# Up weights in whole rows with 512-column matmuls, and each expert's down product after its successor's gate and up products

## Chip, cores and metric

One core of one Trainium2 chip runs the whole layer as one program. The metric is the device time of one execution in microseconds. A change under about 0.5% (8 us) can't be told from none.

## What is computed

One trunk layer: token mixing (mLSTM and GLA scans, an input and an output projection), then expert-choice routed SwiGLU experts. The change touches only the experts. From the reference, cut:

```python
aff = jax.nn.softmax(jnp.einsum('bnd,de->bne', h, w_router).astype(jnp.float32), axis=-1)
g, idx = lax.top_k(jnp.swapaxes(aff, 1, 2), cap)          # cap = 128 tokens for each of 16 experts
xin = jax.vmap(lambda hb, ib: hb[ib])(h, idx)
hid = jax.nn.silu(jnp.einsum('becd,edf->becf', xin, w_gate)) * jnp.einsum('becd,edf->becf', xin, w_up)
y = jnp.einsum('becf,efd->becd', hid, w_down) * g[..., None].astype(h.dtype)
return jax.vmap(lambda yb, ib: jnp.zeros((n, d), h.dtype).at[ib.reshape(-1)].add(yb.reshape(-1, d)))(y, idx)
```

Model width and expert width are 1024. Each expert so has three fp32 matrices of 4 MB, 12 MB in all, and works on 128 tokens, one tile of partitions.

## The kernel before

Every product is made of three fp32r matmuls: each operand is split in a high part (a copy in fp32r) and a low part (operand less high part), and high x high, high x low and low x high are summed in PSUM. The token side is stationary (128x128), the weights move through.

**Units.** An expert's weights come in 12 units of 1 MB (`EU = 12`): units 0 to 3 are gate, 4 to 7 up, 8 to 11 down. Gate and down units are 256 whole rows of the matrix (2 rows of 4 KB for a partition). An up unit is 256 columns of all 1024 rows (8 pieces of 1 KB for a partition). SyncE (SP) loads unit u of the next expert into `e_raw[u]` as soon as TensorE has used unit u of this one; the semaphore `w_used` counts used units. There are 12 raw buffers, so a load has 12 units of time before its own matmuls.

**Splits.** ScalarE (ACT) copies a unit to its high part (`e_split_hi`, L958) into one of 4 buffers (`EH = 4`), so it must wait until the unit four places earlier was used. VectorE (DVE) then writes the low part over the raw unit (`e_split_lo`, L1440). Both run in an order that is written out by hand (`expert_act`, `expert_dve`).

**TensorE's order** (`expert_pe`, L1846): gate units (48 matmuls of 512 columns, L1829), up units (96 matmuls of 256 columns, L1820 to L1822, one quarter of the hidden width per unit), in between the transposes of finished quarters of `hid` (L1843, 8 in all), the 8 transposes of the next expert's tokens (L1836), then the down units (48 matmuls of 512 columns). A quarter of `hid` is multiplied by its up product as soon as its unit is done (`hid_part`), transposed, and split (`hd_hi_part`, `hd_lo_part`), while TensorE works on the next quarter. At the end ACT scales the result into `y_exp` (L989).

**GpSimd (POOL)** gathers the next expert's tokens by an indirect DMA and adds each result to the accumulator in DRAM by another (`scatter`); `y_taken` tells that `y_exp` may be written again. After the last scatter the accumulator is read back, normalised and added to the stream.

The loop over experts is a hardware loop of 15 rounds with the last expert written behind it. The order of an expert in TensorE's program is

```python
for u in range(4):
    e_unit(e, u, xt_hi, xt_lo, e_ps(0))
for q in range(4):
    e_unit(e, 4 + q, xt_hi, xt_lo, quarter(2, q))
    if q:
        hid_transposes(e, q - 1)
if not last:
    x_transposes(e + 1)
hid_transposes(e, 3)
pe.wait_ge(y_free, e + 1)
for u in range(8, EU):
    pe.wait_ge(hd_ok, 4 * e + u - 8 + 1)
    e_unit(e, u, hd_hi, hd_lo, e_ps(4))
```

Of the kernel before, what the change touches and what calls it, by code (L numbers as in the profile page):

```python
# [97 lines left out]
EH = 4  # L98


def build(nc, I, out):

    ctx = ExitStack()
    with ctx:
# [352 lines left out]
        def _(sp):  # L457
# [52 lines left out]
            def expert_src(e, u):  # L510
                if 4 <= u < 8:
                    c = slice(UW * (u - 4), UW * (u - 3))
                    return I["w_e_up"][ds(e, 1), :, c].rearrange("o (k p) n -> p (o k) n", p=P)
                w = I["w_e_gate"] if u < 4 else I["w_e_down"]
                r = 2 * P * (u % 4)
                return w[ds(e, 1), r:r + 2 * P, :].rearrange("o (k p) n -> p (o k) n", p=P)

            def load_expert_unit(e, u):
                dst = e_raw[u][:].rearrange("p (k n) -> p k n", k=KC if 4 <= u < 8 else 2)
                sp.dma_start(dst, expert_src(e, u)).then_inc(e_full[u], 16)  # L520
# [37 lines left out]
        def _(pool):  # L558
# [103 lines left out]
        def _(act):  # L662
# [292 lines left out]
            def e_split_hi(e, u):  # L955
                act.wait_ge(e_full[u], 16 * e + 16)
                act.wait_ge(w_used, EU * e + u + 1)
                act.activation(e_hi[u % EH][:], e_raw[u][:], ACT.Copy).then_inc(e_hi_ok, 1)  # L958

# [4 lines left out]
            def hd_hi_part(e, q):  # L964
                act.wait_ge(hd_mm, 4 * e + q + 1)
                act.activation(hd_hi[:, 2 * q:2 * q + 2, :], quarter(0, q).rearrange("p (k n) -> p k n", k=2), ACT.Copy).then_inc(hd_hi_ok, 1)

            def e_split_his(e, units):
                for u in units:
                    e_split_hi(e, u)  # L970

            def expert_act(e, last):
                act.wait_ge(w_used, EU * e + 4 + EH)
                act.activation(hid[:], e_ps(0), ACT.Silu).then_inc(sg_ok, 1)
                e_split_his(e, (7, 8))
                hd_hi_part(e, 0)
                e_split_hi(e, 9)
                hd_hi_part(e, 1)
                e_split_hi(e, 10)
                hd_hi_part(e, 2)  # L980
                if not last:
                    xt_hi_part(e + 1)
                hd_hi_part(e, 3)
                e_split_hi(e, 11)
                if not last:
                    e_split_his(e + 1, range(3))
                act.wait_ge(w_used, EU * e + EU + EH)
                act.wait_ge(y_taken, e + 1)
                act.activation(y_exp[:], e_ps(4), ACT.Copy, scale=gates[:, ds(e, 1)]).then_inc(y_free, 1)  # L989
                if not last:  # L990
                    e_split_his(e + 1, range(3, 7))
# [9 lines left out]
            e_split_his(0, range(EH, 7))
            with act.Fori(0, N_EXP - 1) as e:
                expert_act(e, False)
            expert_act(N_EXP - 1, True)
# [10 lines left out]
        def _(dve):  # L1015
# [431 lines left out]
            def hid_part(e, q):  # L1447

                if q == 0:
                    dve.wait_ge(sg_ok, e + 1)  # L1450
                dve.wait_ge(w_used, EU * e + 4 + q + 1 + EH)
                h = hid[:, UW * q:UW * (q + 1)]
                dve.tensor_tensor(h, h, quarter(2, q), ALU.mult).then_inc(hid_ok, 1)

            def hd_lo_part(e, q):
                dve.wait_ge(hd_hi_ok, 4 * e + q + 1)
                dve.tensor_tensor(hd_lo[:, 2 * q:2 * q + 2, :], quarter(0, q).rearrange("p (k n) -> p k n", k=2),
                                  hd_hi[:, 2 * q:2 * q + 2, :], ALU.subtract).then_inc(hd_ok, 1)

            def e_split_los(e, units):  # L1460
                for u in units:
                    e_split_lo(e, u)

            def expert_dve(e, last):
                hid_part(e, 0)
                e_split_lo(e, 7)
                hid_part(e, 1)
                e_split_lo(e, 8)
                hd_lo_part(e, 0)
                hid_part(e, 2)  # L1470
                e_split_lo(e, 9)
                hd_lo_part(e, 1)
                hid_part(e, 3)
# [470 lines left out]
```

## Time and profile before

| | us |
|---|---|
| median of 3 runs | 1591.79 |
| lowest and highest | 1586.74, 1592.2 |
| the profiled execution | 1591.46 |
| its span, first to last instruction | 1589.7 |
| expert stage, TensorE's first to last matmul of experts | 979.6 to 1544.6 |

The profile is of one execution; its times are us from the start of its span. "PEclk" or the granted clock is the share of TensorE's full 2.4 GHz that it was given; the other level is 0.5, or 1.2 GHz. PE is TensorE's matmuls, PEld its weight loads. The chain of waits follows the work that ended last back through what released each step, so a stall of TensorE shows in it as a step of another engine or of a DMA. A DMA share over 1 comes from packets that overlap on an engine.

### The profile page before, as it was taken

How to read it: one execution, taken by the hardware profiler on the slowest of the kernel's cores; microseconds unless marked ns; L12 is line 12 of the kernel's file. 1: busy time of each engine (PE TensorE's matmuls, PEld its weight loads, DVE VectorE, ACT ScalarE, POOL GpSimd, SP SyncE). 2: the span in 40 equal slices, each digit the busy share in tenths (PEclk: the TensorE clock that was granted, in tenths of full speed). 3: DMA queues.
4: the chain of work that ended last, by engine and by line, in shares of the span. 5: the costliest groups of instructions: out<-in, count | busy, mean ns of one | idle time of the engine just before them, and what ended most of it. 6: DMA issues, size and time to landing. Idle time of an engine off the chain costs nothing.

```text
span 1589.7 us, 21961 instructions
## 1 busy us (share of the span) xinstructions
PE 1344.7 (85%) x8140; PEld 1180.9 (74%) x8140; DVE 1023.0 (64%) x1325; ACT 765.1 (48%) x853; POOL 103.7 (7%) x121
## 2 busy tenths in 40 slices
PE   4786999899699998178789934999999999999980
PEld 1775889789589997057468823998888889988870
DVE  5637431299534461666734466888888888888855
ACT  5624321133210112466422231877878788787742
POOL 1000000110000000100200001000001000000103
PEclk9998999999899999579799966999999999999995
DMA  9911023000353342000031192999999999999965
GB/s 343 262 38 37 27 62 98 0 1 0 106 185 107 107 133 106 0 1 0 1 119 40 40 331 89 351 380 375 374 374 378 374 373 381 380 380 380 375 199 222
DMA packets 151506, 299.21 MB, mean 188 GB/s; under 512 B 4816, under 2 KB 104144, under 8 KB 149472
## 3 DMA queue, kind: packets, MB, share of 16 engines
q1 hardware_dynamic: 144688, 273.34, 47.4%
q0 software_dynamic: 6768, 25.17, 6.3%
q8 instruction: 36, 0.59, 0.1%
q14 instruction: 14, 0.11, 0.0%
HBM read 277.52 MB, written 29.36 MB: 193 GB/s over the span
## 4 chain that ended last, share of the span: by engine, by line
PE 38%; issue 12%; DVE 2%; DMA 2%; ACT 1%; SPq 1%; POOL 1%; POOLq 0%; DVEq 0%; ACTq 0%
PE psum L1829 21%; PE psum L1822 4%; PE psum L1821 4%; PE psum L1820 4%; PE psum L1707 1%; PE psum L1715 1%; SPq L520 1%; PE psum L1726 1%; PE psum L1725 1%; PE psum L1836 1%; DMA e_raw<-w_e_up 1%; PE psum L1843 1%; PE psum L1741 1%; DVE ht_f L1296 1%; POOL diag L629 1%
## 5 line engine op out<-in xcount | busy, mean ns | idle before, releaser
L1440 DVE TENSOR_TENSOR e_lo<-e_raw,e_hi 128x2048 fp32r<-128x2048 f32 x192 | 434.1, 2287 | 47.5 <-ACT e_hi L958 46.4
L958 ACT ACTIVATE e_hi<-e_raw 128x2048 fp32r<-128x2048 f32 x192 | 362.7, 1913 | 65.5 <-PE psum L1829 50.0
L1613 PE MATMUL psum<-w_hi,h_hi 128*128 128x256 f32 x576 | 165.3, 287 | 0.5 <-issue 0.5
L1615 PE MATMUL psum<-w_lo,h_hi 128*128 128x256 f32 x576 | 164.5, 286 | 0.0
L1614 PE MATMUL psum<-w_hi,h_lo 128*128 128x256 f32 x576 | 164.5, 286 | 0.0
L1820 PE MATMUL psum<-e_hi,xt_hi 128*128 128x256 f32 x512 | 147.3, 288 | 0.0
L1822 PE MATMUL psum<-e_lo,xt_hi 128*128 128x256 f32 x512 | 144.8, 283 | 0.0
L1821 PE MATMUL psum<-e_hi,xt_lo 128*128 128x256 f32 x512 | 144.7, 283 | 0.0
L1613 PEld LDWEIGHTS psum<-w_hi,h_hi 128*128 128x128 f32 x576 | 112.2, 195 | 0.6 <-issue 0.6
L1614 PEld LDWEIGHTS psum<-w_hi,h_lo 128*128 128x128 f32 x576 | 112.3, 195 | 0.0
L1615 PEld LDWEIGHTS psum<-w_lo,h_hi 128*128 128x128 f32 x576 | 112.1, 195 | 0.0
L1821 PEld LDWEIGHTS psum<-e_hi,xt_lo 128*128 128x128 f32 x512 | 98.1, 192 | 0.6
L1820 PEld LDWEIGHTS psum<-e_hi,xt_hi 128*128 128x128 f32 x512 | 97.9, 191 | 0.6
L1572 PE MATMUL psum<-h_hi,w_hi 128*128 128x512 f32 x224 | 72.5, 406 | 30.4 <-DVE kT L1117 14.0
L1822 PEld LDWEIGHTS psum<-e_lo,xt_hi 128*128 128x128 f32 x512 | 97.9, 191 | 0.0
L1829 PE MATMUL psum<-e_hi,xt_hi 128*128 128x512 f32 x256 | 80.0, 394 | 2.5 <-DVE xt_lo L1444 2.5
L1829 PE MATMUL psum<-e_hi,hd_hi 128*128 128x512 f32 x256 | 80.3, 395 | 0.0
L1829 PE MATMUL psum<-e_hi,xt_lo 128*128 128x512 f32 x256 | 79.7, 393 | 0.0
L1829 PE MATMUL psum<-e_lo,xt_hi 128*128 128x512 f32 x256 | 79.7, 393 | 0.0
L1829 PE MATMUL psum<-e_lo,hd_hi 128*128 128x512 f32 x256 | 79.0, 390 | 0.0
L1829 PE MATMUL psum<-e_hi,hd_lo 128*128 128x512 f32 x256 | 78.9, 389 | 0.0
L1572 PE MATMUL psum<-h_lo,w_hi 128*128 128x512 f32 x224 | 71.4, 400 | 0.0
(352 smaller groups left out, 2619.8 us busy)
## 6 DMA issues: line engine op xcount, KB each, us to landing
e_raw<-w_e_gate SPq DMA_DIRECT2D x64, 1024.0 KB, 16.2
e_raw<-w_e_up SPq DMA_DIRECT2D x64, 1024.0 KB, 13.5
e_raw<-w_e_down SPq DMA_DIRECT2D x64, 1024.0 KB, 13.3
ada_x<-w_ada SPq DMA_DIRECT2D x16, 1024.0 KB, 5.3
raw<-w_in_units SPq DMA_DIRECT2D x15, 1024.0 KB, 4.9
ada_raw<-w_ada SPq DMA_DIRECT2D x8, 1024.0 KB, 12.1
xs<-x SPq DMA_DIRECT2D x4, 1024.0 KB, 13.9
acc_dram<-zero_r SPq DMA_DIRECT2D x1, 4096.0 KB, 19.0
```

Source lines behind the costliest of these rows:

```text
L520: sp.dma_start(dst, expert_src(e, u)).then_inc(e_full[u], 16)
L629: pool.tensor_tensor(diag[:], ident[:].unsqueeze(1).to_broadcast([P, KC, P]), vec_c[:, q, :].unsqueeze(2).to_broadcast([P, KC, P]), ALU.mu ...
L958: act.activation(e_hi[u % EH][:], e_raw[u][:], ACT.Copy).then_inc(e_hi_ok, 1)
L1440: dve.tensor_tensor(e_lo[u][:], e_raw[u][:], e_hi[u % EH][:], ALU.subtract).then_inc(e_lo_ok, 1)
L1572: last = pe.matmul(t_lat(s)[:, BANK * q:BANK * (q + 1)], w[m][:, k, c], h[:, k, CTX + BANK * q:CTX + BANK * (q + 1)], start=a, stop=z)
L1613: pe.matmul(o, x_hi[:, k, c], w_hi[n % 2][:, k, :], start=k == 0, stop=False)
L1614: pe.matmul(o, x_lo[:, k, c], w_hi[n % 2][:, k, :], start=False, stop=False)
L1615: last = pe.matmul(o, x_hi[:, k, c], w_lo[n % 2][:, k, :], start=False, stop=k == KC - 1)
L1820: pe.matmul(o, x_hi[:, k, :], hi[:, c], start=k == 0, stop=False)
L1821: pe.matmul(o, x_lo[:, k, :], hi[:, c], start=False, stop=False)
L1822: i = pe.matmul(o, x_hi[:, k, :], lo[:, c], start=False, stop=k == KC - 1)
L1829: i = pe.matmul(o[:, BANK * b:BANK * (b + 1)], x[:, k, :], w[:, D * j + BANK * b:D * j + BANK * (b + 1)], start=a, stop=z)
```

## The change

Up units become pairs of whole rows as gate and down have, and their matmuls get 512 columns. With that, the up product is finished only with its last unit, so there are no quarters any more: `hid` is multiplied, transposed and split in one piece each. TensorE's order is turned: gate and up of expert e, token transposes of e + 1, down of e - 1, `hid` transposes of e. Expert 0 has no down before it and stands ahead of the loop; the last expert's down stands behind it. The loads follow the order of use, and the scatter of expert e is issued behind the gather of e + 3 where it was e + 1.

```diff
             def expert_src(e, u):
-                if 4 <= u < 8:
-                    c = slice(UW * (u - 4), UW * (u - 3))
-                    return I["w_e_up"][ds(e, 1), :, c].rearrange("o (k p) n -> p (o k) n", p=P)
-                w = I["w_e_gate"] if u < 4 else I["w_e_down"]
+                w = (I["w_e_gate"], I["w_e_up"], I["w_e_down"])[u // 4]
...
-            with sp.Fori(0, N_EXP - 1) as e:
-                for u in range(EU):
-
-                    sp.wait_ge(w_used, EU * e + u + 1 + EH)
+            for u in range(8):
+                sp.wait_ge(w_used, u + 1 + EH)
+                load_expert_unit(1, u)
+            with sp.Fori(1, N_EXP - 1) as e:
+                for u in range(8):
+                    sp.wait_ge(w_used, EU * e - 4 + u + 1 + EH)
                     load_expert_unit(e + 1, u)
+                for u in range(8, EU):
+                    sp.wait_ge(w_used, EU * e - 4 + u + 1 + EH)
+                    load_expert_unit(e, u)
+            for u in range(8, EU):
+                sp.wait_ge(w_used, EU * (N_EXP - 1) - 4 + u + 1 + EH)
+                load_expert_unit(N_EXP - 1, u)
...
-            with pool.Fori(1, N_EXP) as e:
+            for e in (1, 2):
                 pool.wait_ge(xt_mm, e)
                 gather(e, tok_g_ok, e)
-                scatter(e - 1)
-            scatter(N_EXP - 1)
+            for e in range(3, N_EXP):
+                pool.wait_ge(xt_mm, e)
+                gather(e, tok_g_ok, e)
+                scatter(e - 3)
+            for e in range(N_EXP - 3, N_EXP):
+                scatter(e)
...
+            def expert_act(e):
+                n = EU * e - 4
+                up_his(e, n + 4)
+                gate_silu(e, n)
+                down_his(e - 1, n + 8)
+                xt_hi_part(e + 1)
+                gate_his(e + 1, n + EU)
+                y_part(e - 1, n + 8)
+                hd_hi_part(e)
...
+            def expert_dve(e):
+                n = EU * e - 4
+                lows(4, n + 4)
+                lows(8, n + 8, range(3))
+                hid_part(e, n)
+                lows(8, n + 8, (3,))
+                xt_lo_part(e + 1)
+                lows(0, n + EU)
+                hd_lo_part(e)
...
+            gate_up(0, 0)
+            x_transposes(1)
+            pe.wait_ge(xt_ok, 2)
+            hid_transposes(0)
+            with pe.Fori(1, N_EXP - 1) as e:
+                n = EU * e - 4
+                gate_up(e, n)
+                pe.wait_ge(hd_ok, e)
+                x_transposes(e + 1)
+                down(e - 1, n + 8)
+                pe.wait_ge(xt_ok, e + 2)
+                hid_transposes(e)
+            last = EU * (N_EXP - 1) - 4
+            gate_up(N_EXP - 1, last)
+            down(N_EXP - 2, last + 8)
+            hid_transposes(N_EXP - 1)
+            down(N_EXP - 1, last + EU)
```

**Two places in the order of the engines.** First ACT, from the last expert's SiLU to the end of the experts; before (L958 is a weight unit's high part with the buffer and raw unit named, L966 the high part of `hid`, L989 the result):

```order
L974 ACTIVATE hid_190<-psum 128x1024 [waits w_used]
L958 ACTIVATE e_hi3_186<-e_raw7_166 128x2048 [waits w_used,e_full7]
L958 ACTIVATE e_hi0_183<-e_raw8_167 128x2048 [waits w_used,e_full8]
L966 ACTIVATE hd_hi_191<-psum 128x256 [waits hd_mm]
L958 ACTIVATE e_hi1_184<-e_raw9_168 128x2048 [waits w_used,e_full9]
L966 ACTIVATE hd_hi_191<-psum 128x256 [waits hd_mm]
L958 ACTIVATE e_hi2_185<-e_raw10_169 128x2048 [waits w_used,e_full10]
L966 ACTIVATE hd_hi_191<-psum 128x256 [waits hd_mm] x2
L958 ACTIVATE e_hi3_186<-e_raw11_170 128x2048 [waits w_used,e_full11]
L989 ACTIVATE y_exp_193<-psum,gates_195 128x1024 [waits y_taken,w_used]
```

The same stretch after the change, in which units 8 to 11 come twice, first those of expert 14 and then those of expert 15:

```order
L978 ACTIVATE hid_190<-psum 128x1024 [waits w_used]
L962 ACTIVATE e_hi0_183<-e_raw8_167 128x2048 [waits w_used,e_full8]
...
L962 ACTIVATE e_hi3_186<-e_raw11_170 128x2048 [waits w_used,e_full11]
L962 ACTIVATE e_hi0_183<-e_raw8_167 128x2048 [waits w_used,e_full8]
L962 ACTIVATE e_hi1_184<-e_raw9_168 128x2048 [waits w_used,e_full9]
L962 ACTIVATE e_hi2_185<-e_raw10_169 128x2048 [waits w_used,e_full10]
L962 ACTIVATE e_hi3_186<-e_raw11_170 128x2048 [waits w_used,e_full11]
L991 ACTIVATE y_exp_193<-psum,gates_195 128x1024 [waits y_taken,w_used]
L986 ACTIVATE hd_hi_191<-psum 128x1024 [waits hd_mm]
L991 ACTIVATE y_exp_193<-psum,gates_195 128x1024 [waits y_taken,w_used]
```

The high part of `hid`, which stood between the down units in quarters, now stands behind all four down units of its own expert and behind the result of the expert before.

Second TensorE, from the end of expert 0's up product onwards (L1829 and L1839 are the matmuls of 512 columns, L1843 and L1852 the `hid` transposes, L1836 and L1846 the token transposes). Before, behind the last quarter's matmuls:

```order
L1843 MATMUL psum<-ident_50,hid_190 128x128 [waits hid_ok]
L1843 MATMUL psum<-ident_50,hid_190 128x128
L1834 ISA
L1836 MATMUL psum<-ident_50,x_tok_187 128x128 [waits gathered]
L1836 MATMUL psum<-ident_50,x_tok_187 128x128 x7
L1840 REGISTER_ALU
L1843 MATMUL psum<-ident_50,hid_190 128x128 [waits hid_ok]
L1843 MATMUL psum<-ident_50,hid_190 128x128
L1815 REGISTER_ALU [waits hd_ok,y_free]
L1829 MATMUL psum<-e_hi0_183,hd_hi_191 128x512 [waits e_lo_ok]
```

and after:

```order
L1839 MATMUL psum<-e_hi3_186,xt_lo_189 128x512 x2
L1846 MATMUL psum<-ident_50,x_tok_187 128x128 [waits gathered]
L1846 MATMUL psum<-ident_50,x_tok_187 128x128 x7
L1852 MATMUL psum<-ident_50,hid_190 128x128 [waits hid_ok,xt_ok]
L1852 MATMUL psum<-ident_50,hid_190 128x128 x7
L1874 UNCONDITIONAL_BRANCH
L1874 ISA
L1832 ISA [waits xt_ok]
L1839 MATMUL psum<-e_hi0_183,xt_hi_188 128x512 [waits e_lo_ok]
```

Before, the down product of expert 0 follows the transposes; after, no matmuls stand between expert 0's up product and expert 1's gate product but the two sets of transposes.

## Rows read from the trace of the kernel before

**Rows 1.** The page: busy totals, and granted clock in 40 slices.

```profile
PE 1344.7 (85%) x8140; PEld 1180.9 (74%) x8140; DVE 1023.0 (64%) x1325; ACT 765.1 (48%) x853; POOL 103.7 (7%) x121
...
PEclk9998999999899999579799966999999999999995
```

**Rows 2.** Windows view: stretch, its us, busy us (instructions), granted clock, DMA share, GB/s.

```profile
1200.00:1400.00 200.00, 200.00 (x1204) 179.16 (x1203) 177.35 (x124) 159.45 (x116) 16.54 (x22) 1.00 1.05 377
```

**Rows 3.** Chain of waits, one expert: start, us, what.

```profile
1212.43 0.22 PE psum L1843 x2
1215.52 0.22 PE psum L1843 x2
1215.74 0.87 PE psum L1836 x8
...
1216.83 21.80 PE psum L1829 x96
...
1251.87 4.34 PE psum L1829 x19
```

**Rows 4.** Groups by form, 1100:1300: busy us, mean ns of one, idle before.

```profile
L1440 DVE TENSOR_TENSOR e_lo<-e_raw,e_hi 128x2048 fp32r<-128x2048 f32 x69 | 156.0, 2287 | 12.8 <-ACT e_hi L958 12.4
L958 ACT ACTIVATE e_hi<-e_raw 128x2048 fp32r<-128x2048 f32 x69 | 130.2, 1913 | 16.6 <-PE psum L1829 16.6
...
L1453 DVE TENSOR_TENSOR hid<-hid,psum 128x256 f32<-128x256 f32 x24 | 10.1, 421 | 10.2 <-PE psum L1822 8.1
...
L1444 DVE TENSOR_TENSOR xt_lo<-psum,xt_hi 128x1024 fp32r<-128x1024 f32 x6 | 7.3, 1214 | 0.0
L989 ACT ACTIVATE y_exp<-psum,gates 128x1024 f32<-128x1024 f32 x6 | 6.7, 1119 | 5.3 <-PE psum L1829 5.3
...
L962 ACT ACTIVATE xt_hi<-psum 128x1024 fp32r<-128x1024 f32 x6 | 6.2, 1028 | 2.9 <-PE psum L1836 2.9
```

**Rows 5.** Windows view: loads of 1 KB pieces, of 4 KB rows, scatter, gather.

```profile
1328.00:1338.00 10.00, 10.00 (x46) 8.29 (x45) 8.05 (x4) 8.01 (x5) 1.78 (x2) 1.00 1.10 348
1341.00:1344.00 3.00, 3.00 (x17) 2.53 (x16) 2.63 (x2) 2.93 (x2) 0.00 (x0) 1.00 1.03 270
1351.00:1353.00 2.00, 2.00 (x20) 2.00 (x19) 1.86 (x4) 1.09 (x2) 0.00 (x0) 1.00 1.03 412
1354.00:1362.00 8.00, 8.00 (x49) 7.12 (x49) 7.87 (x8) 6.32 (x6) 0.00 (x0) 1.00 1.03 410
```

**Rows 6.** Timeline of SP's load issues: start, us, what.

```profile
1336.93 9.56 SPq L520 DMA_DIRECT2D e_raw<-w_e_gate  x4
...
1483.16 8.97 SPq L520 DMA_DIRECT2D e_raw<-w_e_gate  x4
```

**Rows 7.** Load issue to landing: one at 985.3, all of 1300:1400.

```profile
e_raw<-w_e_gate SPq DMA_DIRECT2D x1, 1024.0 KB, 5.0
...
DMA to landing us min/median/max: 11.6/19.1/21.4
```

**Rows 8.** Chain of waits, last two experts.

```profile
1462.08 21.79 PE psum L1829 x96
...
1508.92 13.87 DMA e_raw<-w_e_up
...
1533.64 10.91 PE psum L1829 x48
```

**Rows 9.** Timeline of PE: first work after a gap, gap in brackets.

```profile
69.01 1.31 PE L1536 MATMUL psum<-ident,xs 128*128 128x128 f32 x10 [2.25 <-ACT h L726]
```

**Rows 10.** Windows view: the clock behind gaps of PE.

```profile
70.40:73.80 3.40, 3.04 (x13) 2.65 (x14) 3.37 (x4) 2.47 (x4) 0.00 (x0) 0.50 1.14 208
84.10:90.80 6.70, 5.69 (x16) 4.72 (x17) 6.63 (x6) 4.41 (x4) 0.00 (x0) 0.50 0.01 1
411.20:415.10 3.90, 3.90 (x11) 3.22 (x12) 3.87 (x2) 0.00 (x0) 0.00 (x0) 0.50 0.02 4
415.10:419.00 3.90, 3.90 (x22) 3.32 (x21) 1.82 (x2) 1.91 (x1) 0.00 (x0) 1.00 0.52 147
```

More of the change, by code:

```diff
@@ L962, in xt_hi_part, with hd_hi_part, y_part @@
                 act.activation(xt_hi[:].rearrange("p k n -> p (k n)"), e_ps(6), ACT.Copy).then_inc(xt_hi_ok, 1)
[L964 to L987, printed above, removed]
+            def hd_hi_part(e):
+                act.wait_ge(hd_mm, e + 1)
+                act.activation(hd_hi[:].rearrange("p k n -> p (k n)"), e_ps(6), ACT.Copy).then_inc(hd_hi_ok, 1)
+            def y_part(e, n):
+                act.wait_ge(w_used, n + 4 + EH)
                 act.wait_ge(y_taken, e + 1)
                 act.activation(y_exp[:], e_ps(4), ACT.Copy, scale=gates[:, ds(e, 1)]).then_inc(y_free, 1)
-                if not last:
-                    e_split_his(e + 1, range(3, 7))
+            def expert_act(e):
[7 more added lines that the diff above has]
+                hd_hi_part(e)
             all_stored(act)
@@ L997, in _ @@
             act.nop().then_inc(y_free, 1)
-            e_split_his(0, range(EH))
+            gate_his(0, 0)
             act.wait_ge(route_ready, 1)
             xt_hi_part(0)
[L1001 to L1004, printed above, removed]
+            up_his(0, 4)
+            gate_silu(0, 0)
+            xt_hi_part(1)
+            gate_his(1, 8)
+            hd_hi_part(0)
+            with act.Fori(1, N_EXP - 1) as e:
+                expert_act(e)
+            last = EU * (N_EXP - 1) - 4
+            up_his(N_EXP - 1, last + 4)
+            gate_silu(N_EXP - 1, last)
+            down_his(N_EXP - 2, last + 8)
+            down_his(N_EXP - 1, last + EU)
+            y_part(N_EXP - 2, last + 8)
+            hd_hi_part(N_EXP - 1)
+            y_part(N_EXP - 1, last + EU)
             for j in range(4):
@@ L1460, in e_split_los @@
[L1460 to L1473, printed above, removed]
-                e_split_lo(e, 10)
-                hd_lo_part(e, 2)
-                if not last:
-                    xt_lo_part(e + 1)
-                hd_lo_part(e, 3)
-                e_split_lo(e, 11)
-                if not last:
-                    e_split_los(e + 1, range(7))
@@ L1483, in _, with hid_part, hd_lo_part @@
-            e_split_los(0, range(3))
-            xt_lo_part(0)
-            e_split_los(0, range(3, 7))
-            with dve.Fori(0, N_EXP - 1) as e:
-                expert_dve(e, False)
-            expert_dve(N_EXP - 1, True)
+            def hid_part(e, n):
+                dve.wait_ge(sg_ok, e + 1)
+                dve.wait_ge(w_used, n + 8 + EH)
+                dve.tensor_tensor(hid[:], hid[:], e_ps(2), ALU.mult).then_inc(hid_ok, 1)
+            def hd_lo_part(e):
+                dve.wait_ge(hd_hi_ok, e + 1)
+                dve.tensor_tensor(hd_lo[:].rearrange("p k n -> p (k n)"), e_ps(6), hd_hi[:].rearrange("p k n -> p (k n)"),
+                                  ALU.subtract).then_inc(hd_ok, 1)
@@ L1490, in _ @@
+            last = EU * (N_EXP - 1) - 4
+            lows(4, last + 4)
+            lows(8, last + 8, range(3))
+            hid_part(N_EXP - 1, last)
+            lows(8, last + 8, (3,))
+            lows(8, last + EU)
+            hd_lo_part(N_EXP - 1)
             for j in range(4):
@@ L1844, in hid_transposes, with gate_up @@
                 i.then_inc(hd_mm, 1)
[L1846 removed]
+            def gate_up(e, n):
                 pe.wait_ge(xt_ok, e + 1)
                 for u in range(4):
[L1849 to L1856 removed]
+                    e_unit(u, n + u, xt_hi, xt_lo, e_ps(0))
+                for u in range(4):
+                    e_unit(4 + u, n + 4 + u, xt_hi, xt_lo, e_ps(2))
@@ L1857, in expert_pe, with down @@
+            def down(e, n):
                 pe.wait_ge(y_free, e + 1)
-                for u in range(8, EU):
-                    pe.wait_ge(hd_ok, 4 * e + u - 8 + 1)
-                    e_unit(e, u, hd_hi, hd_lo, e_ps(4))
+                pe.wait_ge(hd_ok, e + 1)
+                for u in range(4):
+                    e_unit(8 + u, n + u, hd_hi, hd_lo, e_ps(4))
             pe.wait_ge(route_ready, 1)
             x_transposes(0)
-            with pe.Fori(0, N_EXP - 1) as e:
-                expert_pe(e, False)
```

94 lines of the change are left out of this document (43 added, 51 removed).

## Prediction

> **What bounds the kernel now.** I read the views in this order. The page's busy totals [rows 1] say little, as they mix all stages: PE 85%, DVE 64%, ACT 48%. The slices show that from 985 us on the granted clock stays full (the last 9s of PEclk), which is the expert stage. A window in that stage [rows 2] shows PE busy for all of its 200 us at clock 1.00, DVE for 177 and ACT for 159, and the DMA engines at a share of 1.05. So TensorE sets the pace, but the DMA has hardly a margin. The chain of waits over one expert [rows 3] holds TensorE alone, without a gap: 96 matmuls of gate and down take 21.80 us (0.2271 each), 8 token transposes 0.87, 8 `hid` transposes 0.87 in four pieces, and the expert lasts 1251.87 - 1216.83 = 35.04 us. That leaves 11.50 for the 96 up matmuls; a single quarter gives the same, 1215.52 - 1212.43 - 0.22 = 2.87 for 24, or 0.1196 each.
>
> Whether the DMA keeps up is read from the loads. From 1336.93 to 1483.16 SP issues four experts' loads [rows 6], 36.56 us for each, slower than TensorE's 35.04. Issue to landing grows from 5.0 us for the first load of the stage to a median of 19.1 around 1350 [rows 7]. This backlog lives on the 12 raw buffers, and runs out only in the last experts: in the chain [rows 8] the last down product starts at 1533.64 and the one two experts earlier at 1462.08, 71.56 us apart, where two experts take 70.08, less 0.87 for token transposes that the last one lacks: 69.21. So 2.4 us are lost to late loads, and the chain goes through a load of an up unit (13.87 us from 1508.92).
>
> **Part 1, up matmuls of 512 columns.** 96 of 256 columns go, 11.50 us, and 48 of the form of gate and down come, 48 x 0.2271 = 10.90. On a TensorE that never waits the whole 0.60 us counts, for 16 experts **-9.6 us**. The number of transposes stays.
>
> **Part 2, up loads of 4 KB rows.** The windows [rows 5] show loads in 1 KB pieces at 348 GB/s and in 4 KB rows at 410, so 3.01 us and 2.56 us for 1 MB. Four units save 1.8 us an expert: 36.6 goes to 34.8 for the DMA. TensorE's new expert is 35.04 - 0.60 = 34.44. The DMA stays behind by 0.4 us an expert, 6 us over the stage, against the 1.5 x 14 = 21 us that the buffers took before the first stall. So the late loads go: **-2.4 us** (between -2.4 and 0).
> The Trainium skill speaks against this part: "DMA: Bandwidth & Descriptors", Specifications, gives 512 B as the smallest transfer for line rate, by which 1 KB and 4 KB rows would load equally fast. Here they don't (348 against 410 GB/s). What the rule would make of the time is rival A.
>
> **Part 3, the turned order, within the loop.** TensorE waits for nothing if each low part is ready before its unit. Set 0 at the start of gate(e); a unit takes 12 x 0.2271 = 2.73 us. Down units start at 22.7, `hid` transposes at 33.6, gate(e + 1) at 34.44. ACT makes a high part (1.91 us [rows 4]) when the unit four places earlier is used; SiLU follows gate at 10.9, the last down high part starts at 21.9 when the last up unit is used. DVE (2.29 a low part) has eleven low parts and this expert's product behind the up units: three down units' low parts done by 24.1, `hid_part` until 25.3, the fourth low part until 27.6 where TensorE needs it at 30.9, xt_lo until 28.8, and gate(e + 1)'s first low part at 31.1, needed at 34.44. The smallest margin is so 3.2 us. DVE's sum is 12 x 2.29 + 3 x 1.21 = 31.1 of 34.44 us, ACT's 12 x 1.91 + 3 x 1.03 + 1.12 = 27.2. `hid_part` over 1024 columns isn't in the trace: 1.21 as xt_lo, at most 4 x 0.42 = 1.68 as four quarters. The margin covers both, so this part costs **0**. Behind `y_part` on ACT stand `hd_hi` and the first up high part, whose parts TensorE reads 17 and 3.3 us after they are done. On POOL the scatter of e - 3 stands behind the gather of e, which has waited for the transposes of the round before; the next gather is needed a whole round later. The new waits of TensorE on `hd_ok` and `xt_ok` end 17 and 5 us before they are reached.
>
> **Part 4, the start.** Here the cover is gone: expert 0 has no down of a predecessor [the second order excerpt]. From the end of up(0) at 0: token transposes until 0.87, xt_hi 1.03 until 2.1 (hand-offs of 0.03 to 0.2 included), xt_lo 1.21 until 3.3; only then may the `hid` transposes write the same PSUM banks, 3.4 to 4.3. ACT makes the first high part of gate(1) behind xt_hi, 2.1 to 4.0, DVE its low part until 6.3; TensorE starts gate(1) at 6.4. The later units come every 2.29 us, faster than the 2.73 they are used in. TensorE waits 2.6 + 2.1 = **+4.7 us** (4 to 6).
>
> **Part 5, the end.** Down(15) follows down(14) with only the `hid` transposes between. Two things meet. The loads of down(15) go into the buffers of down(14), each when its unit is used, which in the loop is 12 units ahead of use and here 4. And ACT has its four high parts in front of `y_part(14)` and of `hd_hi(15)` [the first order excerpt]; `hd_hi(15)` is what TensorE waits for. From the end of down(14) at 0: the last load is issued, and the DMA has nothing else, so it lands at 5.0 [rows 7]; its high part until 6.9, y_part 1.12 until 8.1, hd_hi 1.03 until 9.1; DVE ends the low part at 9.2, hd_lo until 10.4; with hand-offs TensorE goes on at 10.9, where its transposes ended at 0.87: **+10.0 us**. Were the load no wait, the high part would end at 2.1 and the gap be 4.9; that is the lower bound, 11.5 with a landing of 6.5 the upper. The scatter of expert 14 has 16 us until y_part(15) writes `y_exp` again, and behind down(15) all is as before.
>
> **The clock.** Before, the stage has no gap. In other stages the clock fell behind gaps: 2.25 us of gap ahead of 69.01 [rows 9], and 70.4 to 73.8 shows 0.50, the 1.2 GHz level; 84.1 to 90.8 also shows 0.50, and 411.2 to 415.1 right behind idle time, where 11 matmuls run in 3.9 us and 22 in the next 3.9 at 1.00 [rows 10]: half the time at this level is lost. At the end I take 3.9 us of low clock behind the 10 us gap, **+2.0** (1.5 to 2.8). At the start the gaps are 2.6 and 2.1 us with 0.9 of transposes between; **+2.0**, between 0 and 3.4 (half of 6.7).
>
> **Sum.** 1591.46 - 9.6 - 2.4 + 4.7 + 10.0 + 2.0 + 2.0 = 1598.2. The profiled execution is 0.3 us under the median of the runs, 1591.79, so nothing is added. The forecast is **+6.4 us, 0.4%**: the saving of 16 experts is given back in two gaps. Differences under 0.5% (8.0 us, so below 1599.8) can't be told from none by such a measurement.
>
> **Rivals.**
> A, slower: the loads stay at 36.56 us an expert. Against 34.44 the DMA falls behind by 2.1 an expert, 32 us in 15; the buffers bear 21, so TensorE loses 11 where before it lost 2.4. Time 1598.2 + 11 = 1609. It decides once an expert's loads take over 34.44 + 21 / 15 = 35.8. Against it stand the 348 and 410 GB/s; for it that gather and scatter (270 GB/s while the scatter runs [rows 5]) stay. Chance 0.08.
> B, slower: a wait in each round, because DVE does its product for `hid` in the middle of the down low parts. It decides when over 3.2 us come on top; 1 us a round then gives 1598.2 + 15 = 1613. For it: DVE is 90% busy and in order. Chance 0.07.
> C, no change: the two gaps are shorter, the clock stays up at the start and the last load doesn't matter: 1598.2 - 2.0 - 5.1 = 1591. Chance 0.15.
> D, faster: both ends are hidden and only the savings stay, 1591.46 - 12.0 = 1579.5. Nothing covers a TensorE that has no other product to run, so 0.05.
> The forecast itself, 1594 to 1603: 0.65, of which 0.2 lies over 1599.8.
>
> **Numbers.** Slower by over 0.5%: 0.08 + 0.07 + 0.20 = 0.35. Within: 0.45 + 0.15 = 0.60. Faster: 0.05. The range takes in the lower half of no case below C and reaches over the forecast to near A: 1590 to 1607. The likeliest case's own is 1594 to 1603.
>
> **What would show it.** An expert's period of 34.4 us with up matmuls 0.227 apart; load issue to landing that stays well under 19 us; a DMA rate in loads of 410 GB/s throughout; two gaps of TensorE on xt_lo and e_lo behind expert 0, 2.6 and 2.1 us; one of 10 us ahead of the last down product, released by hd_lo (L1477) with hd_hi behind a load of down; clock 0.50 behind both. Wrong would be: a period over 34.6 (A if it grows late and ACT waits for loads, B if from the first round), or an end gap of 5.

## The result

Eleven runs of the changed kernel have a median of 1598.73 us (1593.02 to 1599.7), eleven of the kernel before on the same chip 1589.64 (1584.26 to 1592.2). The ratio is 1.0056 with a 95% interval of 1.0042 to 1.0069: slower by 9 us, on the edge of what the measurement can tell from nothing. The profiled execution took 1598.76 us, the forecast was 1598.2. The ratio is formed over all the runs and can differ from the quotient of the medians, by up to 0.1% in the table of experiments.

### The profile after

The page, with the same lines as [rows 1]:

```profile
PE 1343.1 (84%) x7372; PEld 1146.5 (72%) x7372; DVE 1019.7 (64%) x1229; ACT 744.4 (47%) x791; POOL 123.2 (8%) x121
...
PEclk9888999999899999579799966999999999999985
```

TensorE has 768 matmuls less and is as busy as before (1343.1 us for 1344.7). The last two digits of the clock, 85 for 95, are a first sign of what happened at the end.

The windows view, as [rows 2] (us, busy us and instructions of PE, PEld, DVE, ACT, POOL, then granted clock, DMA share, GB/s), and the landings of the same stretch as in [rows 7]:

```profile
1200.00:1400.00 200.00, 200.00 (x932) 166.56 (x931) 178.79 (x88) 154.20 (x94) 27.36 (x24) 1.00 1.03 398
```

```profile
DMA to landing us min/median/max: 6.4/8.0/8.7
```

TensorE still never waits within the loop. The DMA engines move 398 GB/s where they moved 377, and a load lands 8.0 us after its issue where it took 19.1: the backlog is gone.

The timeline of SP, as [rows 6] (start, us, what):

```profile
1430.43 8.51 SPq L512 DMA_DIRECT2D e_raw<-w_e_gate  x4
1464.87 8.51 SPq L512 DMA_DIRECT2D e_raw<-w_e_gate  x4
```

An expert takes 1464.87 - 1430.43 = 34.44 us, and the issues of loads keep exactly TensorE's pace.

The waits of TensorE between 975 and 1560 us (the engine and what waited, the releaser: us in total, times, longest):

```profile
PE psum L1839 <- DVE hd_lo L1477: 9.6, 1, 9.6
...
PE psum L1852 <- DVE xt_lo L1467: 2.4, 1, 2.4
PE psum L1839 <- DVE e_lo L1463: 1.8, 1, 1.8
```

The first is the end, the other two are the start. The only ones left out stand ahead of expert 0's first product, 11.0 us on its tokens and 2.4 on their low part, and the kernel before has both (10.9 and 2.5 us). The timeline of PE shows the three in their places, the gap in brackets. First the start:

```profile
1004.92 1.03 PE L1846 MATMUL psum<-ident,x_tok 128*128 128x128 f32 x8
1008.32 1.09 PE L1852 MATMUL psum<-ident,hid 128*128 128x128 f32 x8 [2.37 <-DVE xt_lo L1467]
1011.19 1.22 PE L1839 MATMUL psum<-e_hi,xt_hi 128*128 128x512 f32 x2 [1.77 <-DVE e_lo L1463]
...
1016.47 0.75 PE L1839 MATMUL psum<-e_hi,xt_hi 128*128 128x512 f32 x2
```

and the end:

```profile
1528.90 1.03 PE L1852 MATMUL psum<-ident,hid 128*128 128x128 f32 x8
1539.57 1.19 PE L1839 MATMUL psum<-e_hi,hd_hi 128*128 128x512 f32 x2 [9.63 <-DVE hd_lo L1477]
...
1542.27 0.67 PE L1839 MATMUL psum<-e_hi,hd_hi 128*128 128x512 f32 x2
```

Why the end's gap is so long stands on ACT's timeline of the same time:

```profile
1525.85 1.92 ACT L962 ACTIVATE e_hi<-e_raw 128x2048 fp32r<-128x2048 f32 x1 [5.66 <-DMA e_raw<-w_e_down]
...
1531.22 1.91 ACT L962 ACTIVATE e_hi<-e_raw 128x2048 fp32r<-128x2048 f32 x1 [0.82 <-DMA e_raw<-w_e_down]
1534.10 1.91 ACT L962 ACTIVATE e_hi<-e_raw 128x2048 fp32r<-128x2048 f32 x1 [0.97 <-DMA e_raw<-w_e_down]
1535.92 1.10 ACT L991 ACTIVATE y_exp<-psum,gates 128x1024 f32<-128x1024 f32 x1
1536.91 1.01 ACT L986 ACTIVATE hd_hi<-psum 128x1024 fp32r<-128x1024 f32 x1
```

Each of the four high parts of the last down product waits for its load. `hd_hi` (L986), which needs none of them, could have run from 1529.93 on, when the transposes are done, and runs at 1536.91. The windows view of the clock behind the gaps:

```profile
1009.90:1016.70 6.80, 5.51 (x13) 4.35 (x14) 6.80 (x4) 5.23 (x4) 0.00 (x0) 0.50 0.12 50
1532.20:1542.30 10.10, 2.73 (x7) 2.18 (x8) 6.24 (x4) 4.76 (x4) 2.86 (x2) 0.50 0.29 66
```

### Where the time went

TensorE's expert stage, first to last matmul, was 564.92 us and is 571.60 (980.42 to 1552.03). The parts of the +6.7, each from the rows above:

| part | forecast | measured |
|---|---|---|
| start: 1011.19 - 1004.92, less 1.74 of transposes | +4.7 | +4.5 |
| end: 1539.57 - 1528.90, less 0.87 of transposes | +10.0 | +9.8 |
| clock, start: 12 matmuls from 1011.19 to 1016.47, 5.28 us for 2.73, and 0.1 in the next two | +2.0 | +2.7 |
| clock, end: 6 matmuls from 1539.57 to 1542.27, 2.70 us for 1.36, and 0.05 | +2.0 | +1.4 |
| up matmuls and late loads, by difference | -12.0 | -11.7 |
| sum | +6.7 | +6.7 |

Outside of the stage the profiled executions differ by 0.6 us: the stage begins 0.8 later, ahead of all that was changed, and what follows it is 0.2 shorter.

### The profile page after: what moved, and what is told of

Read it like the earlier page. It is cut to its first block, busy times and chain, and to the rows that moved or that the text cites. A ratio compares the mean times of both kernels' runs of the same rounds, so it can differ in the third digit from the quotient of the medians.

```text
span 1597.0 us, 19922 instructions
## 1 busy us (share of the span) xinstructions
PE 1343.1 (84%) x7372; PEld 1146.5 (72%) x7372; DVE 1019.7 (64%) x1229; ACT 744.4 (47%) x791; POOL 123.2 (8%) x121
## 4 chain that ended last, share of the span: by engine, by line
issue 38%; DMA 9%; PE 5%; POOL 4%; DVE 2%; ACT 1%; POOLq 0%; DVEq 0%
DMA acc_dram<-y_exp,tok_s 8%; POOL tok_s L640 1%; PE psum L1724 1%; POOL x_tok L636 1%; PE psum L1732 1%; PE psum L1743 1%; PE psum L1742 1%; POOL tok_g L633 1%; PE psum L1758 1%; DVE ht_f L1317 1%; POOL diag L629 1%; DVE acc L1514 0%; DMA acc<-acc_dram 0%; DVE ssq L1510 0%; ACT wo_hi L899 0%
## 5 line engine op out<-in xcount | busy, mean ns | idle before, releaser
L1463 DVE TENSOR_TENSOR e_lo<-e_raw,e_hi 128x2048 fp32r<-128x2048 f32 x192 | 439.3, 2291 | 70.5 <-ACT e_hi L962 68.9
L962 ACT ACTIVATE e_hi<-e_raw 128x2048 fp32r<-128x2048 f32 x192 | 367.6, 1918 | 135.0 <-PE psum L1839 126.6
L1839 PE MATMUL psum<-e_hi,xt_hi 128*128 128x512 f32 x512 | 161.3, 396 | 4.2 <-DVE xt_lo L1467 2.4
L1839 PE MATMUL psum<-e_hi,xt_lo 128*128 128x512 f32 x512 | 159.6, 393 | 0.0
L1839 PE MATMUL psum<-e_lo,xt_hi 128*128 128x512 f32 x512 | 159.5, 393 | 0.0
L1839 PEld LDWEIGHTS psum<-e_hi,xt_hi 128*128 128x128 f32 x512 | 96.4, 191 | 24.1 <-DVE xt_lo L1467 2.8
L1839 PEld LDWEIGHTS psum<-e_hi,xt_lo 128*128 128x128 f32 x512 | 97.2, 190 | 20.6
L1839 PEld LDWEIGHTS psum<-e_lo,xt_hi 128*128 128x128 f32 x512 | 97.2, 190 | 20.5
L1839 PE MATMUL psum<-e_hi,hd_hi 128*128 128x512 f32 x256 | 80.8, 397 | 9.6 <-DVE hd_lo L1477 9.6
L1839 PE MATMUL psum<-e_hi,hd_lo 128*128 128x512 f32 x256 | 79.4, 391 | 0.0
L1839 PE MATMUL psum<-e_lo,hd_hi 128*128 128x512 f32 x256 | 79.4, 391 | 0.0
L1589 PE MATMUL psum<-h_hi,w_lo 128*128 128x512 f32 x224 | 71.0, 398 | 0.0
L1047 DVE TENSOR_TENSOR w_lo<-raw,w_hi 128x2048 fp32r<-128x2048 f32 x15 | 34.3, 2289 | 55.8 <-ACT w_hi L685 55.7
L1589 PEld LDWEIGHTS psum<-h_hi,w_hi 128*128 128x128 f32 x224 | 39.1, 195 | 37.7 <-issue 27.6
```

The source lines that it names most:

```text
L1047: dve.tensor_tensor(lo[:], (ada_raw[n] if n < 8 else raw[n % 2])[:], hi[:], ALU.subtract).then_inc(lo_ready, 1)
L1589: last = pe.matmul(t_lat(s)[:, BANK * q:BANK * (q + 1)], w[m][:, k, c], h[:, k, CTX + BANK * q:CTX + BANK * (q + 1)], start=a, stop=z)
L1839: i = pe.matmul(o[:, BANK * b:BANK * (b + 1)], x[:, k, :], w[:, D * j + BANK * b:D * j + BANK * (b + 1)], start=a, stop=z)
```

## Experiments

The runs of each table line are compared with the kernel before on the same chip (medians 1589.87, 1589.83 and 1591.2 for the three groups); "stage" is TensorE's first to last matmul of experts in the profiled execution.

| run | median us | ratio (95%) | stage us |
|---|---|---|---|
| changed kernel again (ctl_after) | 1598.47 | 1.0052 (1.0035 to 1.0069) | 571.54 |
| kernel before again (ctl_before) | 1589.88 | 0.9982 (0.9967 to 0.9997) | 563.55 |
| e1: `hd_hi` behind one high part | 1588.6 | 1.0002 (0.9985 to 1.0019) | 562.38 |
| e2: last loads in free buffers | 1591.81 | 1.0014 (0.9996 to 1.0032) | 565.93 |
| e3: end covered | 1585.48 | 0.998 (0.9963 to 0.9996) | 558.95 |
| e4: start covered | 1591.21 | 1.0019 (1.0001 to 1.0038) | 565.79 |
| e5: e3 and e4 | 1580.9 | 0.9942 (0.992 to 0.9963) | 554.27 |
| e6: up matmuls of 256 columns | 1605.72 | 1.01 (1.0078 to 1.0123) | 579.35 |
| e7: up loads in 1 KB pieces | 1602.54 | 1.0081 (1.0057 to 1.0104) | 575.92 |
| e8: kernel before, up loads in rows | 1589.36 | 0.9982 (0.9969 to 0.9996) | 562.41 |
| e9: rows and 512 columns, order of before | 1661.29 | 1.0446 (1.0432 to 1.0461) | 634.26 |

**The two controls.**

> The changed kernel itself, as a control beside the others of this chip: ratio to before 1.004 to 1.007.

> The kernel before itself, for a second trace of it: whether its expert stage again lasts 564.9 us from first to last expert matmul and loses some 2.4 us to late loads in the last experts. Ratio 1.000. If the stage is 562 to 563, the profiled execution of before was one with more late loads than the median.

The changed kernel repeats its 9 us. The kernel before, against itself, comes out 0.18% faster with an interval that leaves out 1: these intervals are too narrow by about that, 3 us, and smaller differences are read from the stage in the traces. Its stage, 563.55 us, lies between the two values that its expectation names.

The stage has a spread of its own. At its opening the clock is low in every trace, behind TensorE's waits for the first tokens, and how long it stays low differs: the first 18 matmuls, which take 4.1 us at the full clock, start within 6.8 us in the kernel before, in the changed kernel and in ctl_after, within 6.1 to 6.2 in ctl_before, e1, e2 and e8, and within 5.8 to 5.9 in e3 to e7 and e9. Two stages can so differ by up to 1.0 us that no edit made. Below this is called the opening.

### The end (e1, e2, e3)

e1 moves `hd_hi` ahead of three of the four high parts:

```diff
-            down_his(N_EXP - 1, last + EU)
+            e_split_hi(N_EXP - 1, 8, last + EU)
             y_part(N_EXP - 2, last + 8)
             hd_hi_part(N_EXP - 1)
+            for u in range(1, 4):
+                e_split_hi(N_EXP - 1, 8 + u, last + EU + u)
```

and likewise `hd_lo` on DVE, behind the first low part.

> Changed kernel with only the end reordered on ACT and DVE: after the first high part of down(15) come y_part(14) and hd_hi(15), then the other three high parts; hd_lo(15) stands behind the first low part. Loads stay as they are. Theory (the 9.6 us gap ahead of down(15) is ACT's order behind the last load): y_part 0.1 to 1.2, hd_hi 2.3, hd_lo 3.5, TensorE on at 3.6, so a gap of 2.7 us in place of 9.6, no low clock or a shorter one, and 7 to 9 us less than the changed kernel, ratio to the kernel before 1.000 to 1.002. Rival (the load itself bounds down(15)): the gap moves behind the first down unit and the time stays within 2 us of the changed kernel.

The timeline of PE in e1, and its window behind the gap:

```profile
1527.83 1.04 PE L1855 MATMUL psum<-ident,hid 128*128 128x128 f32 x8
1531.42 0.70 PE L1842 MATMUL psum<-e_hi,hd_hi 128*128 128x512 f32 x2 [2.55 <-DVE hd_lo L1479]
```

```profile
1528.00:1540.00 12.00, 9.45 (x45) 7.60 (x44) 8.79 (x5) 7.44 (x5) 1.74 (x2) 1.00 0.64 188
```

The gap falls from 9.6 to 2.55 us and the clock stays at 1.00, the 2.4 GHz level. Three high parts and low parts placed later take back all that the change had lost. The stage is 9.2 us shorter: 7.1 of the gap, 1.4 of the clock behind it, 0.6 of the opening.

e2 leaves the order and loads the last down units into buffers 0 to 3, which have long been free:

```diff
-            for u in range(8, EU):
+            for u in range(4):
                 sp.wait_ge(w_used, EU * (N_EXP - 1) - 4 + u + 1 + EH)
-                load_expert_unit(N_EXP - 1, u)
+                sp.dma_start(e_raw[u][:]..., expert_src(N_EXP - 1, 8 + u)).then_inc(e_full[u], 16)
```

> Changed kernel in which down(15) is loaded into raw buffers 0 to 3, free since gate(15), 20 us earlier; orders stay. Theory: the last high part no longer waits for a load, only for its buffer: done at 2.1, y_part 3.2, hd_hi 4.3, hd_lo 5.5 behind the low part that ends at 4.4, TensorE on at 5.6: a gap of 4.7 us, 5 us less than the changed kernel, clock still low behind it. Rival (the gap is the order alone, not the load): gap stays 9 to 10 us and the time too.

ACT's and PE's timelines in e2:

```profile
1528.97 1.91 ACT L962 ACTIVATE e_hi<-e_raw 128x2048 fp32r<-128x2048 f32 x1 [0.81 <-PE psum L1839]
...
1531.79 1.01 ACT L986 ACTIVATE hd_hi<-psum 128x1024 fp32r<-128x1024 f32 x1
```

```profile
1534.44 0.72 PE L1839 MATMUL psum<-e_hi,hd_hi 128*128 128x512 f32 x2 [4.69 <-issue]
```

Now the last high part waits for TensorE, 0.81 us, and no longer for a load; what is left of the gap is the high part, `y_part` and `hd_hi` in a row. So the gap of 9.6 us is 4.9 of load and 4.7 of order; the forecast had 4.9 for the gap "were the load no wait". The two are not additive: with `hd_hi` moved forward (e1), the load is off the path too.

e3 takes e2's buffers and puts the `hid` transposes of expert 15 in the middle of down(14), with `xt_hi` and `xt_lo` as a second pair of `hd` tiles:

```diff
             for u in range(4):
+                if u == 2:
+                    hid_transposes(N_EXP - 1)
                 e_unit(8 + u, last + 8 + u, hd_hi, hd_lo, e_ps(4))
-            hid_transposes(N_EXP - 1)
             pe.wait_ge(hd_ok, N_EXP)
```

> Changed kernel with the end covered: down(15) loaded early into raw buffers 0 to 3, its hid transposes between down(14)'s second and third unit, its parts written over xt_hi and xt_lo, its product in the PSUM banks of gate. Theory: no gap of TensorE from expert 1 to the end, clock full, 9.6 + 2.4 = 12 us less than the changed kernel, about 1587, ratio to before 0.998. Rival (the changed kernel loses its time elsewhere than in the gap, or the scatter of expert 14 takes its place and holds y_exp): 4 us or more of it come back.

```profile
1522.00 1.04 PE L1861 MATMUL psum<-ident,hid 128*128 128x128 f32 x8
1522.79 0.71 PE L1848 MATMUL psum<-e_hi,hd_hi 128*128 128x512 f32 x2
```

These two rows of its PE timeline carry no bracket: the gap is gone. The stage is 12.6 us shorter than the changed kernel's: 9.8 and 1.4 for gap and clock are 11.2 of it, 1.0 is the opening. The other 0.5 comes from the start, where the low clock fell earlier and so caught fewer of the wide matmuls. The second gap there is 1.28 us for 1.77 only because the transposes ahead of it ran slower by as much.

### The start, and both (e4, e5)

e4 puts expert 1's token transposes into the middle of up(0), the first high and low parts of gate(1) ahead of the token parts, and the `hid` transposes into a free bank pair:

```diff
-            gate_up(0, 0)
-            x_transposes(1)
-            pe.wait_ge(xt_ok, 2)
-            hid_transposes(0)
+            ...
+            for u in range(4):
+                if u == 2:
+                    x_transposes(1)
+                e_unit(4 + u, 4 + u, xt_hi, xt_lo, e_ps(2))
+            pe.wait_ge(hid_ok, 1)
+            ... the transposes of hid, into e_ps(4)
```

> Changed kernel with only the start changed: token transposes of expert 1 before up(0)'s third unit, hid transposes of expert 0 into the free down banks (so they don't wait for xt_lo), three high parts and two low parts of gate(1) ahead of the end of up(0). Theory: in place of gaps of 2.4 and 1.8 us two of at most 1.5, 2.3 us less, and 3.4 more if the clock then stays at 1.00 (it was 0.50 for 6.8 us behind them): 2 to 6 us less than the changed kernel. Rival (the clock's fall is not from these gaps): only 2.3 us less, 0.50 still there.

e5 is e3 and e4 together.

> Changed kernel with the covered end and the new start together. Theory: the steady saving of 0.6 us an expert is then all that is left beside a start of under 3 us: 1598.7 - 12 - 2 to 6 = 1581 to 1585, ratio to before 0.994 to 0.997, 16 experts from first to last matmul 551 to 556 us. Rival (the saving of 9.6 us isn't real): not below before.

The PE timeline of e4 at the start, the window there, and TensorE's only wait in e5 from 985 us on:

```profile
1006.29 1.09 PE L1886 MATMUL psum<-ident,hid 128*128 128x128 f32 x8 [1.38 <-DVE hid L1477]
```

```profile
1004.00:1018.00 14.00, 12.49 (x58) 9.99 (x58) 12.44 (x8) 9.71 (x7) 0.63 (x1) 1.00 0.89 339
```

```profile
PE psum L1895 <- DVE hid L1483: 1.4, 1, 1.4
```

One gap is left in both, the 1.38 us in which DVE makes its product for `hid`; e4's window shows 1.00 around it. e4's stage is 5.8 us shorter. 5.3 of it come from the start: from the end of up(0) at 1004.74 to gate(1) at 1007.50 pass 2.76 us, or 1.9 less 0.87 of transposes, where the changed kernel has 4.5, and 2.7 more for the low clock. 0.9 are the opening, and the low clock at the end took 0.3 more. e5 takes 8.9 us less than the kernel before (0.9942, interval under 1): the saving that the change aimed at was there all the time, and the changed kernel lost it in two places, at the first and at the last round of the loop.

### The parts that save (e6, e7, e8)

e6 is the changed kernel with up matmuls of 256 columns, but for those that start or end a sum:

```diff
-                        for b in range(2):
+                        c = UW if 4 <= u < 8 and not (a or z) else BANK
+                        for b in range(D // c):
```

> Changed kernel with the up matmuls again of 256 columns, but for the first and last of each bank: 88 of 256 and 4 of 512 in place of 48 of 512 an expert. Theory: 88 x 0.1196 + 4 x 0.2271 = 11.43 us against 10.90, a period of 34.98 in place of 34.45, 8.5 us more than the changed kernel. Rival (columns make no difference where the number of columns is the same): within 2 us.

Its SP timeline gives the period:

```profile
1431.93 8.51 SPq L512 DMA_DIRECT2D e_raw<-w_e_gate  x4
1466.98 8.51 SPq L512 DMA_DIRECT2D e_raw<-w_e_gate  x4
```

35.05 us for 34.44. Over twelve experts the period is 35.04 against 34.45 (the same loads from 1046.55 to 1466.98 here, from 1051.44 to 1464.87 in the changed kernel), so 0.58 an expert and 9.3 in sixteen, a little over the 8.5 expected. The stage is only 7.8 longer because the low clock took less in this trace, 0.9 at the opening and 0.8 behind the start's gaps. The first part of the forecast is settled.

e7 loads the up units in 1 KB pieces again:

```diff
+                if 4 <= u < 8:
+                    c = slice(UW * (u - 4), UW * (u - 3))
+                    return I["w_e_up"][ds(e, 1), :, c].rearrange("o (k p) n -> p (o k) n", p=P)
...
-                dst = e_raw[u][:].rearrange("p (k n) -> p k n", k=2)
+                dst = e_raw[u][:].rearrange("p (k n) -> p k n", k=KC if 4 <= u < 8 else 2)
```

> Changed kernel with the up units loaded in pieces of 1 KB again (the up weights then lie in other places than the matmuls take them from, so the product is of other numbers; amounts and instructions are the same). Theory: the DMA needs 36.4 us an expert against 34.45 of TensorE, landings grow from 5 to over 20 us, and TensorE waits from about the tenth expert on; 15 x 2 - 21 = 9 us more than the changed kernel, and the end gap of 9.6 gets longer if the backlog reaches it. Rival (1 KB and 4 KB load equally fast, or the DMA doesn't matter here): landings stay at 8 us and the time is within 1 us.

Its SP timeline, TensorE's waits and the window 1300 to 1500 us:

```profile
1186.87 8.51 SPq L515 DMA_DIRECT2D e_raw<-w_e_gate  x4
1221.32 9.06 SPq L515 DMA_DIRECT2D e_raw<-w_e_gate  x4
...
1475.58 8.08 SPq L515 DMA_DIRECT2D e_raw<-w_e_gate  x4
```

```profile
PE psum L1842 <- DVE e_lo L1466: 5.3, 4, 1.4
```

```profile
1300.00:1500.00 200.00, 195.95 (x910) 162.08 (x909) 171.31 (x85) 147.87 (x91) 30.48 (x20) 1.00 1.05 380
```

Until 1221 us the issues come every 34.45 us; the next seven take 254.26, or 36.3 each. That is rival A at work, and it comes late, as foreseen: the wait on e_lo has three gaps of 1.3 to 1.4 us at 1409.8, 1446.0 and 1482.1 besides the one of the start. But the loss is small: the stage is 4.4 us longer than ctl_after's, or 5.4 without the 1.0 that this trace lost less at the opening, and not 9 to 11. The end gap, 9.4 us, did not grow with the backlog. The rate was right (36.3 for 36.56); the reserve was not. By 1267 us the landings have grown from 4.7 to 19.9 us, and until 1475.58 the issues fall back 254.26 - 7 x 34.45 = 13.1 us: some 28 us behind, of which TensorE lost 5. By this estimate the buffers bear some 23 us, where the forecast took 21 from the kernel before, whose backlog (1.5 x 14) had only just been used up. And 28 us is less than the 32 that the forecast let the loads fall behind.

e8 does the other half, the kernel before with up loads in whole rows:

```diff
-                if 4 <= u < 8:
-                    ...
-                w = I["w_e_gate"] if u < 4 else I["w_e_down"]
+                w = (I["w_e_gate"], I["w_e_up"], I["w_e_down"])[u // 4]
...
-                dst = e_raw[u][:].rearrange("p (k n) -> p k n", k=KC if 4 <= u < 8 else 2)
+                dst = e_raw[u][:].rearrange("p (k n) -> p k n", k=2)
```

> The kernel before with the up units loaded as whole rows of 4 KB, matmuls and order as before (each up unit so holds other numbers than its matmuls take it for; amounts and instructions are the same). Theory: the loads take 34.8 us an expert and fit under TensorE's 35.04; landings stay under 10 us, the 2.4 us of late loads are gone and nothing else changes: 2 to 2.5 us less than before, ratio 0.998 to 0.999. Rival (late loads cost the median run nothing): ratio 1.000.

TensorE's waits from 985 us on and the landings of 1300 to 1400 us, first in the kernel before again, then in e8:

```profile
PE psum L1843 <- DVE hid L1453: 1.5, 1, 1.5
```

```profile
DMA to landing us min/median/max: 18.2/19.3/20.6
```

```profile
PE psum L1840 <- DVE hid L1450: 0.3, 1, 0.3
```

```profile
DMA to landing us min/median/max: 5.5/7.5/8.9
```

The backlog vanishes by the loads in whole rows alone. What it had cost is seen in one gap at 1531 us, 1.5 us in the control's trace, 1.6 in the first and 0.3 here. The chain of waits gives the whole: from the down product two experts earlier to the last one are 71.56 us in the first trace [rows 8], 70.87 in the control's and here, by its rows,

```profile
1461.95 21.79 PE psum L1826 x96
...
1531.67 10.93 PE psum L1826 x48
```

69.72. So late loads had cost 1.8 and 1.2 us. The stage is 1.1 us shorter than the control's, with the same opening, and 2.5 shorter than the first trace's, of which 0.7 is the opening. The expected 2 to 2.5 us can't be seen in the medians (1589.36 and 1589.88), and the ratio of 0.9982 is the one that the control has too. Neither e7 nor e8 tells the length of the pieces from their places: the 1 KB pieces of an up unit also lie 4 KB apart in DRAM, where whole rows lie side by side.

### The turn (e9)

e9 has rows and 512 columns in the order of the kernel before, so that `hid` is multiplied, transposed and split in one piece with nothing of another expert beside it:

```diff
                 for q in range(4):
-                    e_unit(e, 4 + q, xt_hi, xt_lo, quarter(2, q))
-                    if q:
-                        hid_transposes(e, q - 1)
+                    e_unit(e, 4 + q, xt_hi, xt_lo, e_ps(2))
                 if not last:
                     x_transposes(e + 1)
-                hid_transposes(e, 3)
+                hid_transposes(e)
...
```

> The kernel before with rows and 512 columns for up, hid in one piece, but each expert's down directly behind its own up. Theory: each expert has the bare chain product 1.2, transposes 0.9, high part 1.0, low part 1.2 with hand-offs against 0.9 of token transposes: TensorE waits about 3 us an expert, 50 us in all, less 9.6 and 2.4, and the clock falls behind some of the gaps for up to 1.7 us each: 1628 to 1656. Rival (ACT and DVE hide it in the turned order as in this one): near the changed kernel.

Its chain of waits over one expert:

```profile
1157.64 1.23 DVE hid L1442
...
1158.91 1.11 PE psum L1817 x8
...
1160.04 1.03 ACT hd_hi L963
...
1161.10 1.24 DVE hd_lo L1446
...
1162.56 34.58 PE psum L1804 x144
...
1202.10 35.74 PE psum L1804 x144
```

From 1157.61 to 1162.56 the chain runs over the product, transposes, high and low part, 4.95 us, of which 0.87 (token transposes beside the product) and 1.11 are TensorE's work: 3.0 idle. Over the stage the waits view has 38.4 us on `hd_lo`, 7.2 on `hid` and 2.4 ahead of the last down product, 48.0 in sixteen experts.

The 144 matmuls behind the idle time would take 32.7 us at the full clock. In the first two rounds they take nearly that:

```profile
1008.01 32.96 PE psum L1804 x144
```

In the thirteen rounds from the third on they take 34.3 to 35.8, with the same idle time ahead of them. The difference is the low clock, 0.50 in this window:

```profile
1163.70:1167.10 3.40, 3.40 (x10) 2.62 (x9) 3.40 (x3) 0.08 (x1) 0.00 (x0) 0.50 0.45 177
```

All fifteen rounds and the last 48 matmuls (12.51 us for 10.90) add up to 30 us over the full clock. So 48.0 + 30 = 78 us of the 81.4 are accounted for that the stage has over 564.9 - 12 = 552.9 (634.26); the `hid` transposes, 1.11 us for 0.87, are most of the rest. The time lies 5 us above the expected range, whose upper end allowed 1.7 us of low clock for each gap, where 1.9 came, and nothing for slower transposes. In this order rows and wide matmuls cost far more than they give; no other order without the turn was tried. The turn avoids that in every round but the first and the last.

## Why the prediction was right

**Up matmuls, -9.6.** Right: period 34.44, and 35.05 with the columns put back (e6).

**Late loads, -2.4.** The mechanism is shown by e7 and e8: landings of 19 us with 1 KB pieces, 8 with rows. The size was read somewhat too large: the working took 71.56 - 69.21 for late loads alone, and e8, whose loads land in 5.5 to 8.9 us, still shows 69.72. So they cost 1.8 us in that trace and 1.2 in ctl_before. The table's difference gives 11.7 - 9.6 = 2.1.

**The turned order, 0.** Right: no wait of TensorE within the loop. Rival B did not come about: the period is 34.45 us in the first rounds (1051.44 to 1085.89) and 34.44 in the last.

**Start, +4.7.** Measured 4.5, by the steps named: xt_lo, then e_lo. e4 shows that the cover was the cause.

**End, +10.0.** Measured 9.8. The working had the last load land 5.0 us after the end of down(14), and then the high part, `y_part` and `hd_hi` in a row. The last high part starts at 1534.10, 5.2 us after that end, and the order is the one foreseen. e1 and e2 tell the halves apart, 4.9 for the load and 4.7 for the order.

**Clock, +2.0 and +2.0.** The sum was right (4.1), but by luck, as the halves were not. At the start it was 2.7: the low clock lasted 6.8 us, which the text had as the upper end. At the end the clock was low for 10.2 us, but 7.4 of those were gap and cost nothing, so 1.4 and not 2.0.

**Rival A, +11.** Its condition did not arise. Where it was made to arise (e7), it cost 4.4 to 5.4 and not 11: two terms of its sum were off, the 21 us taken for the reserve of the buffers, which is some 23, and the 32 us of falling behind, which came to some 28.
The rule of the Trainium skill that spoke for it ("DMA: Bandwidth & Descriptors", Specifications: line rate from 512 B on) doesn't hold for these loads: in the same kernel 200 us of stage move 380 GB/s with up units in 1 KB pieces (e7) and 397 with rows, and only the first builds up a backlog. Whether the length of the pieces or their places make the difference, no run here shows.

**The chances and the level.** Most chance lay on "within 0.5%", and the ratio is 0.56%. The forecast step was +6.4 us, the medians differ by 9.1. The terms are not to blame (+6.7 in the stage, as forecast). It is the basis: the profiled execution of the kernel before, 1591.46, lies 1.8 us above the median of its eleven runs. The executions spread over 8 us, and the median of the three shown (1591.79) lies 2.2 above that of the eleven, over a quarter of the bound of 8 us between "same" and "slower". The time itself was met by luck in part: the basis was 1.8 us above the median of the kernel before, and the changed kernel's profiled execution lies at its own median (1598.76 and 1598.73). The second trace of the kernel before (stage 563.55) is 1.4 us shorter in the expert stage, 0.7 by the opening and 0.7 by less late loads (70.87 for 71.56). Whether this is what sets the median of eleven runs below the first trace stays open.

## To carry to other kernels

Turning a loop's order so that one item's chain hides behind the next one's work moves the exposed chain to the first and the last round; write down what each engine has queued there, since code behind a loop that keeps the loop's order can put a needed short instruction behind four that wait for loads (moving three high parts behind it was worth some 9 us of 1598 here). When the distance between a buffer's release and its next use falls at the end, from 12 units to 4 here, load into buffers that are already free. And count idle time of TensorE with the low clock behind it: in e9 it added some 30 us to 48 of idle time. Before a difference of 1 us between two stages is explained, look whether the low clock at their start lasted equally long.

## What was not expected of the hardware

The clock does not follow the length of a gap alone. A gap of 2.55 us (e1) and one of 1.38 (e4, e5) left it at 1.00. In the changed kernel, with gaps of 2.37 and 1.77 us around eight transposes, it fell within the second gap and was 0.50 for 6.8 us. In e3 it fell already during the transposes, which take 1.58 us for 1.09, behind a gap of 2.37 us and ahead of one of 1.28:

```profile
1007.36 1.58 PE L1861 MATMUL psum<-ident,hid 128*128 128x128 f32 x8 [2.37 <-DVE xt_lo L1473]
```

In e9 the same idle time, 0.4 and 2.56 us around the transposes, left the clock at 1.00 in the first two rounds and brought it down in the thirteen behind them. A gap of 4.69 us (e2) brought 3.4 us of low clock, which began 0.5 us after the restart. The rows of e2's PE timeline show it, pairs of matmuls first 0.83 us apart, from 1538.85 on 0.47:

```profile
1534.98 1.04 PE L1839 MATMUL psum<-e_lo,hd_hi 128*128 128x512 f32 x2
1535.81 1.06 PE L1839 MATMUL psum<-e_hi,hd_lo 128*128 128x512 f32 x2
...
1538.85 0.62 PE L1839 MATMUL psum<-e_hi,hd_hi 128*128 128x512 f32 x2
1539.32 0.63 PE L1839 MATMUL psum<-e_lo,hd_hi 128*128 128x512 f32 x2
```

So neither the length of a gap nor the sum of two tells what the clock will do, and what a gap costs does not grow with it: 1.4 us of clock behind 9.6 of gap, 2.7 behind 4.1. What decides stays open in these runs.
